# A bidirectional encoder layer on eight cores: two halves in residue order against one pass of three stages in token order

## The chip, the cores and the metric

The kernel runs on all 8 NeuronCores of one Trainium2 chip. Every core works on 4096 tokens of its own and recomputes what it needs of its neighbours' tokens: its window of x has 6144 rows, 1024 of them halo on each side. No data passes between cores. The metric is the device time in microseconds of the slowest core.

## The reference

```python
hn = rmsnorm(x, norm_g)
q, k, v, z_a, hc, gb, gc, z_b, g = split(hn @ w_in)      # widths 3 x 1536, then 5 x 512, then 2048
for gi, dil in enumerate((1, 4, 16)):                    # 8 heads of 64 per group
    # each query sees the keys at distances dil * j, |j| <= 64, with an ALiBi bias
    out[gi], lse[gi] = banded_attention(q, k, v, dil)
attn = sum(softmax(lse)[gi] * out[gi])
a = (silu(z_a) * attn) @ w_attn_out                      # 512 -> 1024
conv = centred depthwise convolution of width 3 of gc * hc
c = (silu(z_b) * gb * conv) @ w_conv_out                 # 512 -> 1024
merged = sigmoid(g_a + b) * a + sigmoid(g_c + b) * c
y = rmsnorm(x + merged @ w_o, final_g)
```

The model width is 1024. The tokens are one sequence of 16384 and two of 8192.

## The kernel before

The kernel is written on the five instruction queues directly. A helper records every instruction with the resources it reads and writes, and puts in the semaphore waits; each engine runs its own list in order. So the order in which the Python code emits instructions is the order on each engine. Most operations of VectorE (DVE), ScalarE (ACT) and GpSimd (POOL) have a line of their own; projections share `proj_fm` (matmul at L373), ACT copies out of PSUM share L366, and all DMAs L176. x tiles and outputs go on SP's queue, the weights, which are cast from f32 to bf16 on the way, on POOL's.

A core handles its 4096 tokens in two halves of 2048. The normalised, transposed window of one half, `hnT` (8 x 4096 columns of bf16), holds the tokens in residue order: tokens with the same remainder modulo 16 stand together, 256 per remainder. Loads of x with a row step of 16 put them there. The stages, once per half, are:

- **Norm** (`p1_stages`): per tile of 128 tokens a load, a square with sum on ACT (`rms_stat`, L385), two small POOL operations, the scaling on DVE (L432), eight transposes on TensorE (L438) and a copy into `hnT`. Half 0 does this for 32 tiles ahead of everything else.
- **Attention** (`phase2`): 12 units, one for each of 4 head pairs and 3 groups. `att_stages` gives each unit eight items: scores (L750), exponential (L758), multiplication with a table of bias and mask (L762), product with values and ones (L780) and accumulation. Between the items the pieces of `proj_pieces` project queries, keys and values for the next unit. Group 2 projects values tile by tile with `hnT` as the stationary operand (L672); groups 0 and 1 project them like keys and transpose them (L618, L692). Group 0 comes first and writes the accumulator, groups 1 and 2 add on DVE. After group 2 `finalize_parts` divides by the denominators and applies the SiLU gate.
- **Convolution** (`phase3a`) and **gates** (`phase3b`): wide projections of 512 columns; results stay in SBUF (`gattn`, `gconv`, `mergedV`).
- **Output** (`p3_stages`): 16 tiles; in half 0 mixed with the norm of the 16 tiles that half 1 still lacks, the other half of `hnT` being moved along by four DVE copies (L1120). Barriers stand before the attention and before the output.

The order of the mixed pipelines comes from times that are written into the code:

```python
return [(0, L), (1, S), (3, N), (6, E)] if h == 0 else [(0, L), (1, S), (3, N), (4.5, E)]
```

Load, square, scaling with transposes, and copy of tile i are issued at i plus these numbers, sorted.

Of the kernel before, what the change touches and what calls it, by code (L numbers as in the profile page):

```python
# [17 lines left out]
WIN = 4096  # L18
LW = 256
XROWS = 6144  # L20
EPS = 1e-6
# [4 lines left out]
X_BYTES = 84224  # L26
NWS = 8
# [8 lines left out]
def _tile_off(g):  # L36
    idx = np.arange(128)
    if g == 0:
        return 16 * (idx % 8) + idx // 8
    if g == 1:  # L40
        return 4 * (idx % 32) + idx // 32
    return idx

def _etab():
    sl = _slopes()
    out = np.zeros((24, 128, 256), np.float32)
    for g in range(3):
# [146 lines left out]

def build_program():
# [12 lines left out]
    cbf_d = nc.dram_tensor("cbf", [128, 512], BF16, kind="ExternalInput")  # L208
    et_d = nc.dram_tensor("etab", [24 * 128, 256], BF16, kind="ExternalInput")
    y_d = nc.dram_tensor("y", [TOK_CORE, D], F32, kind="ExternalOutput")  # L210

    import contextlib
    es = contextlib.ExitStack()
    with es:
# [888 lines left out]
        for f_ in first_loads:  # L1103
            f_()
# [130 lines left out]
```

How the kernel before makes its waits and increments, by code:

```python
                def body(e):  # L1153
                    for (wl, fn, tok, inc) in E.prog:
                        wl2 = [(sem[sname], rank[sname][v] if sname in rank else v) for (sname, v) in wl]
                        emb = None
                        if EMBED_WAIT and wl2 and kind in EMBED_WAIT and inc != 16:
                            emb = wl2.pop()
                        for (sh, v) in wl2:
                            e.wait_ge(sh, v)
                        ins = fn(e)
                        if emb is not None:
                            ins._wait_ge(emb[0], emb[1])
                        if tok is not None:
                            if tok[0] in rank:
                                if tok[1] in rank[tok[0]]:
                                    ins.then_inc(sem[tok[0]], 1)
                            else:
                                ins.then_inc(sem[tok[0]], inc)
                    if kind == "sp":
                        for sname, v in final_waits.items():
                            e.wait_ge(sem[sname], v)
                        for k2 in ("pe", "act", "dve", "pool"):
                            E2 = B.engs[k2]
                            if E2.count:
                                e.wait_ge(sem[E2.semname], rank[E2.semname][E2.count])
```

The softmax here doesn't subtract the row's maximum and nothing guards it: scores larger than these inputs give would overflow.

## Time and profile before

| | |
|---|---|
| time, median of 3 runs | 1803.38 us (1803.29 to 1804.26) |
| span of the profiled execution, slowest core | 1800.1 us |
| spans of the eight cores | 1783.9 to 1800.1 us |
| TensorE busy | 1632.2 us (91%) |
| VectorE busy | 954.4 us (53%) |
| ScalarE busy | 737.0 us (41%) |
| DMA, mean over the span | 62 GB/s |

The span goes from the first to the last instruction on the slowest core; the time of a run also holds what lies around it, 3.3 us between this span and the median. PE is TensorE's matmul side, PEld its weight loads, which overlap the matmuls. The end of a matmul is modelled in the profile, so starts are the safer thing to read in it.

### The profile page before, as it was taken

The page shows a single profiled execution, that of the slowest core. Times are in us where ns is not written, and L with a number is a line of the kernel's source. Part 1 is how long each engine was busy: PE and PEld are TensorE (multiplying, and loading weights), DVE is VectorE, ACT ScalarE, POOL GpSimd, SP SyncE. Part 2 cuts the span into 40 slices and gives each one's busy share as a digit, 9 for nine tenths or more (in the row PEclk, how much of TensorE's full clock was granted, in tenths as well). Part 3 has the DMA queues.
Part 4 walks back from the last instruction along what each step waited for, and adds up shares of the span by engine and source line. Part 5 has one row for each costly group of instructions (what it writes and reads, how often), then busy time and mean ns, then how long its engine had stood idle before and what let it go on. Part 6 is the DMA issues. An engine that isn't in the chain of part 4 may idle for free.

```text
span 1800.1 us, 30600 instructions; the slowest of 8 cores (1783.9 to 1800.1 us)
## 1 busy us (share of the span) xinstructions
PE 1632.2 (91%) x12270; PEld 894.3 (50%) x12328; DVE 954.4 (53%) x1490; ACT 737.0 (41%) x1385; POOL 246.7 (14%) x328
## 2 busy tenths in 40 slices
PE   2699999999897999999777998998999899999997
PEld 2356556556564444444333564565655644444443
DVE  4724654835748564433662347366474675633446
ACT  5654563564544112222353635546356421122222
POOL 5700010000100111000343000001000010100011
PEclk9999999999998999999998999999999999999999
DMA  9731041321311453221999313204204143522248
GB/s 257 180 46 19 10 48 19 36 21 13 36 19 30 53 47 36 24 24 30 253 284 127 34 13 39 25 7 50 20 3 46 13 65 36 48 24 27 34 123 275
DMA packets 177838, 112.23 MB, mean 62 GB/s; under 512 B 152480, under 2 KB 158752, under 8 KB 177696
## 3 DMA queue, kind: packets, MB, share of 16 engines
q0 software_dynamic: 154176, 46.15, 25.8%
q1 hardware_dynamic: 23520, 64.12, 11.6%
q8 instruction: 97, 1.59, 0.4%
q14 instruction: 45, 0.37, 0.1%
HBM read 139.61 MB, written 16.78 MB: 87 GB/s over the span
## 4 chain that ended last, share of the span: by engine, by line
PE 70%; DVE 10%; DMA 8%; ACT 5%; issue 4%; POOL 2%; SPq 0%; POOLq 0%; ACTq 0%; DVEq 0%
PE ps L373 52%; PE ps L672 6%; PE ps L1050 6%; DMA X<-xw 5%; PE ps L780 4%; DMA y<-X 3%; PE ps L750 2%; DVE X L839 2%; ACT X L758 2%; POOL stat L390 1%; DVE X L762 1%; ACT X L366 1%; DVE X L795 1%; DVE X L844 1%; DVE X L841 1%
## 5 line engine op out<-in xcount | busy, mean ns | idle before, releaser
L373 PE MATMUL ps<-hnT,wbf 128*128 128x512 bf16 (+4 forms) x5488 | 1096.3, 354 | 9.3 <-DVE X L834 3.9
L373 PEld LDWEIGHTS ps<-hnT,wbf 128*128 128x128 bf16 x5504 | 499.8, 99 | 528.2 <-issue 28.1
L762 DVE TENSOR_TENSOR X<-X,et 128x512 bf16<-128x512 bf16 x384 | 159.1, 424 | 317.5 <-ACT X L758 300.5
L366 ACT ACTIVATE X<-ps 128x512 bf16<-128x512 f32 (+3 forms) x384 | 194.7, 512 | 296.0 <-PE ps L373 281.4
L176 POOL DMA_DIRECT2D wbf<-w_in x144 | 132.0, 925 | 1156.0 <-PE ps L373 916.2
L758 ACT ACTIVATE X<-ps 128x512 bf16<-128x512 f32 x384 | 207.5, 598 | 118.3 <-PE ps L750 116.4
L780 PE MATMUL ps<-X 128*128 128x128 bf16 x1536 | 119.6, 222 | 45.7 <-DVE X L762 32.7
L385 ACT ACTIVATE X<-X 128x1024 bf16<-128x1024 f32 x80 | 84.3, 1053 | 117.4 <-DMA X<-xw 66.9
L487 PE MATMUL ps<-wbf,X 128*128 128x512 bf16 x500 | 116.4, 389 | 13.3 <-DVE X L1076 7.2
L780 PEld LDWEIGHTS ps<-X 128*128 128x128 bf16 x1536 | 89.7, 99 | 71.4 <-DVE X L762 41.5
L1064 ACT ACTIVATE X<-ps,cf 128x512 f32<-128x512 f32 x64 | 44.1, 690 | 181.8 <-DVE X L1073 108.9
L672 PE MATMUL ps<-wbf,hnT 128*128 128x128 bf16 x2048 | 118.3, 219 | 0.0
L672 PEld LDWEIGHTS ps<-wbf,hnT 128*128 128x128 bf16 x2048 | 115.7, 98 | 1.9
L1073 DVE SCALAR_TENSOR_TENSOR X<-X,ps 128x512 f32<-128x512 f32 x64 | 43.7, 683 | 136.3 <-PE ps L1050 136.3
L438 PE MATMUL ps<-cbfs,X 128*128 128x128 bf16 x384 | 43.7, 284 | 70.3 <-DVE X L432 66.2
L487 PEld LDWEIGHTS ps<-wbf,X 128*128 128x128 bf16 x512 | 50.4, 100 | 74.2 <-issue 14.0
L750 PE MATMUL ps<-X 64*128 64x128 bf16 x1536 | 76.8, 220 | 10.0 <-ACT X L758 9.2
L390 POOL TENSOR_TENSOR stat<-stat,cf 128x1 f32<-128x1 f32 x80 | 75.2, 940 | 18.3 <-DVE cf L306 11.7
L438 PEld LDWEIGHTS ps<-cbfs,X 128*128 128x128 bf16 x384 | 33.2, 128 | 84.1 <-ACT X L385 25.8
L1070 DVE SCALAR_TENSOR_TENSOR X<-X,ps 128x512 f32<-128x512 f32 x64 | 43.8, 684 | 56.7 <-PE ps L1050 56.7
L676 DVE CAST X<-ps 128x512 bf16<-128x512 f32 x64 | 44.3, 692 | 55.6 <-PE ps L672 55.6
L987 ACT ACTIVATE X<-ps 128x512 f32<-128x512 f32 x32 | 19.1, 597 | 132.2 <-PE ps L373 81.6
(60 smaller groups left out, 1234.3 us busy)
## 6 DMA issues: line engine op xcount, KB each, us to landing
X<-xw SPq DMA_DIRECT2D x80, 512.0 KB, 7.9
wbf<-w_in POOLq DMA_DIRECT2D x144, 256.0 KB, 6.2
y<-X SPq DMA_DIRECT2D x32, 512.0 KB, 6.6
wbf<-w_o POOLq DMA_DIRECT2D x16, 256.0 KB, 4.2
et<-etab SPq DMA_DIRECT2D x24, 128.0 KB, 2.2
X<-w_ao POOLq DMA_DIRECT2D x2, 1024.0 KB, 9.9
X<-w_co POOLq DMA_DIRECT2D x2, 1024.0 KB, 9.6
X<-gvec SPq DMA_DIRECT2D x2, 512.0 KB, 9.5
```

Of the source, the lines that this page charges most:

```text
L176: E.prog.append((wl, lambda e: e.dma_start(out=out, in_=in_), tok, 16))
L366: return op("act", lambda e: e.activation(out=out, in_=in_, func=AF.Copy), reads=reads, writes=writes)
L373: fns.append(lambda e, kt=kt: e.matmul(bv.cols(0, n), lhsT=w_lhsT(s, kt), rhs=hnT.ap(kt * WIN + rhs_start, rhs_dims), start=(kt == 0), sto ...
L385: op("act", lambda e: e.activation(out=junk_ap, in_=src_ap, func=AF.Square, accum_out=stat.cols(c0, 1)), reads=[src_res], writes=[junk_res ...
L390: op("pool", lambda e: e.tensor_tensor(out=stat.cols(c0 + 2, 1), in0=stat.cols(c0 + 1, 1), in1=cf.cols(CF_MH, 1), op=ALU.pow), reads=[r, R ...
L487: fns.append(lambda e, dt_=dt_, nh=nh, bv=bv: e.matmul(bv.cols(0, 512), lhsT=mergedV.cols(dt_ * NOWN + r16 * 128, 128), rhs=wbf.cols(dt_ * ...
L672: fns.append(lambda e, tt=tt, kt=kt, p0=p0: e.matmul(bv.cols(tt * 128, 128), lhsT=hnT.cols(kt * WIN + p0, 128), rhs=w_lhsT(sv, kt), start= ...
L750: fns.append(lambda e, b2=b2, t=t, kt_=kt_, bi=bi, bv=bv, hh=hh: e.matmul(bv.cols(b2 * 256 + t * 128, 128), lhsT=ktV[par].cols(kt_ * 128, ...
L758: op("act", lambda e, bv=bv, hh=hh: e.activation(out=prv.cols(hh * 512, 512), in_=bv.cols(0, 512), func=AF.Exp, scale=0.125), reads=[R_ban ...
L762: op("dve", lambda e, hh=hh, eoff=eoff: e.tensor_tensor(out=prv.ap(hh * 512, [[256, 2], [1, 256]]), in0=prv.ap(hh * 512, [[256, 2], [1, 25 ...
L780: fns.append(lambda e, b2=b2, t=t, kt_=kt_, hh=hh: e.matmul(bv.cols(hh * 256 + b2 * 128, 128), lhsT=vbV[par].cols(kt_ * VB_T + 64 * hh, 12 ...
L1050: fns.append(lambda e, ct=ct: e.matmul(bv.cols(0, 512), lhsT=wv.cols(ct * D + dt_ * 128, 128), rhs=gv_.cols(ct * NOWN + cc * 512, 512), st ...
```

## The change

`hnT` grows to the core's whole window, 8 x 6144 columns in natural token order, and every stage runs once over all of it.

1. **Norm with convolution.** 48 norm tiles in the order 7 to 40, 0 to 6, 41 to 47. The convolution is cut into 32 steps (`conv_step`, 4 channel tiles by 8 chunks of 512 tokens), and after each step `p1_until` issues a stretch of the norm's instructions, 1.36 tiles' worth. Each step projects HC, GC, ZB and GB; SiLU is now one ACT function. The result goes to DRAM (`gc_s`).
2. **Attention by head pair.** 24 units: head pair, then half, then group 2, 1, 0. `hnT` being in token order, the permutation by residue now happens where ACT copies queries and keys out of PSUM (strided reads or writes), and values of all groups are projected tile by tile with a strided `hnT` operand as stationary weights: step 1, 4 or 16 elements. Keys and values that both halves of a head pair need are computed in half 0, saved to DRAM (`k_s`, `v_s`) and loaded in half 1. Group 2 comes first and its accumulator write is an ACT copy with a step of 16; groups 1 and 0 add on DVE. The gated result goes to DRAM (`ga_s`). The pieces of the next unit are spread evenly over the eight items.
3. **Gates and output.** 8 chunks of 512 tokens: per chunk the gated arrays are loaded from DRAM and eight `merge_step`s run, each two gate projections (2 x 8 matmuls) and two branch projections (2 x 4), over a ring of six banks. Between them, one chunk behind, one output tile after every second step (`out_mm`: 16 matmuls into banks 6 and 7, then the DVE sum and the norm). The last four output tiles stand alone at the end. All 16 gate weight blocks stay in SBUF, and `w_o` is loaded once.

The barriers, the value transposes, the moving copies and the second half's reload of convolution, gate and output weights are gone. The stages of the old form are all removed; here are the core lines of the new one, moved left:

```diff
+    ga_d = nc.dram_tensor("ga_s", [4 * 128, TOK_CORE], BF16)
+    gc_d = nc.dram_tensor("gc_s", [4 * 128, TOK_CORE], BF16)
+    KOV = (1, 4, 16)
+    k_d = [nc.dram_tensor("k_s%d" % g, [128, KOV[g] * 128], BF16) for g in range(3)]
+    v_d = [nc.dram_tensor("v_s%d" % g, [128, KOV[g] * VB_T], BF16) for g in range(3)]
...
+order = list(range(7, 41)) + list(range(0, 7)) + list(range(41, 48))
...
+    return [(0, 0, L), (1, 1, S), (2.2, 2, N), (3, 3, E)]
...
+def p1_until(t):
+    while p1pos["i"] < len(p1ev) and p1ev[p1pos["i"]][0] <= t:
+        p1ev[p1pos["i"]][3]()
+        p1pos["i"] += 1
...
+    b_hc, b_gc, b_zb, b_gb = abank(), abank(), abank(), abank()
+    proj_fm(b_hc, w_hc, s, 512)
+    act_copy(hcs.v.base, bank(b_hc).cols(0, 512), [R_bank[b_hc]], hcs.r)
+    proj_fm(b_gc, w_gc, s, 512)
+    op("dve", lambda e: e.tensor_tensor(out=U.v.cols(2, 512), in0=bank(b_gc).cols(0, 512), in1=hcs.v.base,
+                                        op=ALU.mult), reads=[R_bank[b_gc]] + hcs.r, writes=U.r)
+    proj_fm(b_zb, w_zb, s, 512)
+    op("act", lambda e: e.activation(out=sz.v.base, in_=bank(b_zb).cols(0, 512), func=AF.Silu),
+       reads=[R_bank[b_zb]], writes=sz.r)
+    proj_fm(b_gb, w_gb, s, 512)
+    op("dve", lambda e: e.tensor_tensor(out=GZ.v.cols(1, 512), in0=bank(b_gb).cols(0, 512), in1=sz.v.base,
+                                        op=ALU.mult), reads=[R_bank[b_gb]] + sz.r, writes=GZ.r)
+    a0 = 1 if c == 0 else 0
+    n = 513 - a0 if c == 7 else 512 - a0
+    cw0, cw1, cw2 = (cf.cols(CF_CW + ct * 3 + k_, 1) for k_ in range(3))
+    cav = ca.v.cols(0, n)
+    op("dve", lambda e: e.tensor_scalar(out=cav, in0=U.v.cols(a0 + 1, n), scalar1=cw1, scalar2=None, op0=ALU.mult),
+       reads=U.r + [R_const], writes=ca.r)
+    op("dve", lambda e: e.scalar_tensor_tensor(out=cav, in0=U.v.cols(a0, n), scalar=cw0, in1=cav,
+                                               op0=ALU.mult, op1=ALU.add), reads=U.r + ca.r, writes=ca.r)
+    op("dve", lambda e: e.scalar_tensor_tensor(out=cav, in0=U.v.cols(a0 + 2, n), scalar=cw2, in1=cav,
+                                               op0=ALU.mult, op1=ALU.add), reads=U.r + ca.r, writes=ca.r)
+    op("dve", lambda e: e.tensor_tensor(out=gcs.v.cols(0, n), in0=cav, in1=GZ.v.cols(a0, n), op=ALU.mult),
+       reads=ca.r + GZ.r, writes=gcs.r)
+    if c < 7:
+        dve_copy(U.v.cols(0, 2), U.v.cols(512, 2), U.r, U.r)
+        dve_copy(GZ.v.cols(0, 1), GZ.v.cols(512, 1), GZ.r, GZ.r)
+    o0 = 512 * c - 1 + a0
+    dma("sp", "d_gc%d" % k, bass.AP(gc_d, ct * 128 * TOK_CORE + o0, [[TOK_CORE, 128], [1, n]]),
+        gcs.v.cols(0, n), reads=gcs.r, writes=R_gcd[max(c - 1, 0):c + 1])
...
+p1_until(0)
+conv_wload(0)
+load_consts()
+dma("sp", "d_gb", gb_.v.base, bass.AP(gvec, 0, [[0, 128], [1, D]]), writes=R_gb)
+p1_until(4)
+conv_wload(1)
+p1_until(6)
+conv_wload(2)
+conv_wload(3)
+p1_until(7)
+stepi = 0
+for sc in range(4):
+    for ct in range(4):
+        for c in (2 * sc, 2 * sc + 1):
+            conv_step(ct, c)
+            stepi += 1
+            if stepi == 1:
+                p1_until(11.5)
+            else:
+                p1_until(11.5 + (stepi - 1) * 1.36)
+        if sc == 3 and ct == 0:
+            wahead(3)
+        if sc == 3 and ct == 1:
+            wahead(4)
+p1_until(1e9)
...
+units = [(hp, h, g) for hp in range(4) for h in range(NHALF) for g in (2, 1, 0)]
...
+        if nload:
+            dma("sp", "d_kl%d" % par, kt.v.cols(0, nload * 128), k_d[g].ap(), reads=[R_kd[g]], writes=ksub(0, nload))
+            dma("sp", "d_vl%d" % par, vb.v.cols(0, nload * VB_T), v_d[g].ap(), reads=[R_vd[g]], writes=vsub(0, nload))
...
+    def vpiece(t0, n):
+        def run():
+            bk = next_pbank()
+            bv = bank(bk)
+            fns = []
+            lo, hi = 10 ** 9, 0
+            wf, wr = w_slot(sv)
+            for tt in range(n):
+                t = t0 + tt
+                if g == 0:
+                    p0 = ks + 128 * t
+                elif g == 1:
+                    p0 = ks + 512 * (t // 4) + t % 4
+                else:
+                    p0 = ks + 2048 * (t // 16) + t % 16
+                lo, hi = min(lo, p0), max(hi, p0 + 127 * d + 1)
+                for kk in range(8):
+                    fns.append(lambda e, tt=tt, kk=kk, p0=p0: e.matmul(
+                        bv.cols(tt * 128, 128), lhsT=hnT.ap(kk * WT + p0, [[d, 128]]),
+                        rhs=wf(kk), start=(kk == 0), stop=(kk == 7)))
+            pe_group(fns, reads=wr + hres(lo, hi), writes=[R_bank[bk]])
+            dve_copy(vb.v.ap(t0 * VB_T, [[VB_T, n], [128, 2], [1, 64]]),
+                     bv.ap(0, [[128, n], [64, 2], [1, 64]]), [R_bank[bk]], vsub(t0, n))
+        return run
+    if g == 0:
+        if h:
+            kl = [kpiece(128 + 512 * c) for c in range(4)]
...
+            kl = [kpiece(512 * c) for c in range(4)] + [kpiece(2048, 128)]
+    else:
+        kl = [kpiece(c) for c in range(nload // 4, nt // 4)]
+    vl = [vpiece(t0, min(4, nt - t0)) for t0 in range(nload, nt, 4)]
+    pieces += kl + vl
...
+    def save_piece():
+        t0 = nt - nov
+        dma("sp", "d_ks%d" % g, k_d[g].ap(), kt.v.cols(t0 * 128, nov * 128), reads=ksub(t0, nov), writes=[R_kd[g]])
+        dma("sp", "d_vs%d" % g, v_d[g].ap(), vb.v.cols(t0 * VB_T, nov * VB_T), reads=vsub(t0, nov), writes=[R_vd[g]])
+    if h == 0:
+        pieces.append(save_piece)
...
+    if g == 2:
...
+        act_copy(av_.ap(4 * quad + 2 * j, [[NOWN, 2], [1, 2], [16, 128]]),
+                 bv.ap(0, [[256, 2], [128, 2], [1, 128]]), [R_bank[ob]], acc_.r)
...
+    if g == 1:
+        av, ares = av_.ap(quad + 1024 * j, [[NOWN, 2], [4, 256]]), acc_.r
+    else:
+        av, ares = av_.ap(512 * quad + 256 * j, [[NOWN, 2], [1, 256]]), acc_res(quad)
...
+def out_tick(last=False):
+    i = done["mm"]
+    out_mm(i)
+    done["mm"] += 1
+    if done["fin"] < i:
+        out_fin(done["fin"])
+        done["fin"] += 1
+    if i + 2 < 32:
+        x3_load(i + 2)
...
+for c in range(8):
...
     for dt_ in range(8):
+        merge_step(c, dt_)
+        if c > 0 and dt_ % 2 == 1:
+            out_tick()
+    if c + 2 < 8:
+        load_chunk(c + 2)
+for _ in range(4):
+    out_tick()
+out_fin(done["fin"])
```

## Rows read from the trace of the kernel before

**Rows 1.** The page: engines' busy time, and TensorE's granted clock in 40 slices.
```profile
PE 1632.2 (91%) x12270; PEld 894.3 (50%) x12328; DVE 954.4 (53%) x1490; ACT 737.0 (41%) x1385; POOL 246.7 (14%) x328
...
PEclk9999999999998999999998999999999999999999
```

**Rows 2.** Windows by stage: length, busy per engine, clock, DMA share, GB/s.
```profile
0.00:82.00 82.00, 32.78 (x257) 24.73 (x258) 50.74 (x50) 52.50 (x81) 58.01 (x76) 1.00 0.83 227
82.00:569.40 487.40, 456.16 (x4357) 277.87 (x4366) 257.01 (x493) 242.37 (x493) 34.53 (x40) 0.98 0.26 28
569.40:859.00 289.60, 283.45 (x1339) 128.60 (x1352) 144.00 (x186) 65.64 (x104) 30.43 (x35) 0.99 0.34 38
859.00:958.80 99.80, 68.65 (x377) 33.18 (x384) 62.90 (x52) 50.11 (x80) 45.41 (x71) 0.90 0.92 264
958.80:1444.90 486.10, 453.83 (x4357) 276.67 (x4366) 256.83 (x492) 241.96 (x492) 35.17 (x41) 0.98 0.29 30
1444.90:1732.40 287.50, 280.95 (x1341) 127.99 (x1354) 144.22 (x186) 66.00 (x105) 30.42 (x35) 0.99 0.35 38
1732.40:1800.10 67.70, 56.43 (x251) 25.24 (x256) 38.68 (x32) 18.40 (x32) 12.72 (x32) 0.93 0.78 256
```

**Rows 3.** TensorE's timeline in attention: start, length, instructions, idle before.
```profile
150.84 0.40 PE L750 MATMUL ps<-X 64*128 64x128 bf16 x8
151.17 0.62 PE L780 MATMUL ps<-X 128*128 128x128 bf16 x8
151.62 5.34 PE L373 MATMUL ps<-hnT,wbf 128*128 128x512 bf16 x24
156.90 0.40 PE L750 MATMUL ps<-X 64*128 64x128 bf16 x8
```

**Rows 4.** Windows of two head pairs (half 0), and of one unit.
```profile
109.43:230.47 121.04, 116.53 (x1112) 70.50 (x1113) 61.52 (x121) 61.56 (x126) 5.28 (x7) 0.99 0.20 22
230.47:350.52 120.05, 113.67 (x1093) 69.18 (x1094) 67.27 (x127) 61.09 (x125) 8.75 (x11) 0.99 0.24 26
186.56:230.47 43.91, 41.06 (x324) 22.30 (x322) 31.27 (x51) 23.50 (x46) 0.03 (x1) 0.96 0.03 10
```

**Rows 5.** TensorE's timeline at the end of half 0's attention.
```profile
541.98 0.62 PE L780 MATMUL ps<-X 128*128 128x128 bf16 x8
...
559.22 1.03 PE L780 MATMUL ps<-X 128*128 128x128 bf16 x8 [4.15 <-DVE X L762]
...
568.56 1.03 PE L780 MATMUL ps<-X 128*128 128x128 bf16 x8 [3.76 <-DVE X L762]
```

**Rows 6.** Groups by form: count, busy us, mean ns, idle before.
```profile
L672 PE MATMUL ps<-wbf,hnT 128*128 128x128 bf16 x2048 | 118.3, 219 | 0.0
...
L672 PEld LDWEIGHTS ps<-wbf,hnT 128*128 128x128 bf16 x2048 | 115.7, 98 | 1.9
...
L432 DVE SCALAR_TENSOR_TENSOR X<-X,stat 128x1024 bf16<-128x1024 f32 x48 | 61.4, 1281 | 12.2 <-POOL stat L390 10.9 <-DMA X<-gvec 1.2
...
L993 DVE TENSOR_TENSOR X<-ps,X 128x512 f32<-128x512 f32 x32 | 22.1, 691 | 1.1
...
L1011 DVE SCALAR_TENSOR_TENSOR X<-X,cf 128x1920 f32<-128x1920 f32 x8 | 17.7, 2218 | 0.3
...
L1009 DVE TENSOR_SCALAR X<-X,cf 128x2048 f32<-128x2048 f32 x8 | 10.3, 1286 | 0.3
```

**Rows 7.** TensorE's timeline in the mixed stage.
```profile
859.41 7.07 PE L487 MATMUL ps<-wbf,X 128*128 128x512 bf16 x32 [3.58 <-DVE X L1076]
871.86 8.55 PE L487 MATMUL ps<-wbf,X 128*128 128x512 bf16 x31 [5.38 <-DVE X L494]
...
949.27 1.01 PE L438 MATMUL ps<-cbfs,X 128*128 128x128 bf16 x8 [4.41 <-DVE X L432]
...
958.85 9.41 PE L373 MATMUL ps<-hnT,wbf 128*128 128x512 bf16 x32 [2.36 <-DMA wbf<-w_in]
```

**Rows 8.** TensorE's timeline at the start.
```profile
20.64 2.14 PE L438 MATMUL ps<-cbfs,X 128*128 128x128 bf16 x16 [20.64 <-DVE X L432]
```

More of the change, by code:

```diff
@@ L193, in barrier, with __init__ @@
         self.epoch = ep
+class Buf:
+    def __init__(self, view, res):
+        self.v = view
+        self.r = res
 def build_program():
@@ L300, in build_program, with mrg @@
+        fgV = View(et_t[:, 0:2048].bitcast(F32))
+        R_mrg = [[Res() for _ in range(8)] for _ in range(2)]
+        def mrg(m, dt_):
+            return hnT.cols(dt_ * WT + m * 512, 512)
         CF_HB, CF_CW, CF_FL, CF_BG, CF_MH = 0, 16, 28, 32, 48
@@ new lines, in wload @@
+        def wload(sname, dst, col, res):
+            src = bass.AP(w_in, col, [[INW, 128], [128 * INW, 8], [1, 128]])
+            dma("pool", sname, dst, src, writes=res)
+        wblocks = []
+        for hp in range(4):
+            for h in range(NHALF):
+                for g in (2, 1, 0):
+                    for c in (C_Q, C_K, C_V):
+                        wblocks.append(c + g * 512 + hp * 128)
+                wblocks.append(C_ZA + hp * 128)
+        for dt_ in range(4):
+            wblocks.append(C_G + dt_ * 128)
+            wblocks.append(C_G + 1024 + dt_ * 128)
@@ L810, in att_stages @@
+                        ov = bv.ap(0, [[256, 2], [1, 256]])
+                        op("dve", lambda e: e.tensor_tensor(out=av, in0=ov, in1=av, op=ALU.add),
+                           reads=[R_bank[ob]] + ares, writes=ares)
                     items.append((stage_a, stage_b))
@@ new lines, in x3_load, with out_mm @@
+        def x3_load(i):
+            s = i % 4
+            dma("sp", "d_x3%d" % s, x3_[s].v.base, bass.AP(xw, (OWN0 + 128 * i) * D, [[D, 128], [1, D]]), writes=x3_[s].r)
+        out_st = {}
+        def out_mm(i):
+            c, r = divmod(i, 4)
+            m = c % 2
+            s = i % 4
+            x3 = x3_[s]
+            for nh in range(2):
+                bv = bank(6 + nh)
+                fns = []
+                for dt_ in range(8):
+                    fns.append(lambda e, dt_=dt_, nh=nh, bv=bv: e.matmul(
+                        bv.cols(0, 512), lhsT=hnT.cols(dt_ * WT + m * 512 + r * 128, 128),
+                        rhs=wo_[dt_].v.cols(nh * 512, 512), start=(dt_ == 0), stop=(dt_ == 7)))
+                pe_group(fns, reads=R_mrg[m] + [x for w_ in wo_ for x in w_.r], writes=[R_bank[6 + nh]])
+            op("dve", lambda e: e.scalar_tensor_tensor(out=x3.v.base, in0=bank(6, 2).base, scalar=0.5,
+                                                       in1=x3.v.base, op0=ALU.mult, op1=ALU.add),
+               reads=[R_bank[6], R_bank[7]] + x3.r, writes=x3.r)
+            out_st[i] = rms_stat(x3.v.base, x3.r)
```

1124 lines of the change are left out of this document (407 added, 717 removed).

## The prediction

> **What bounds the kernel now.** I first read the page. TensorE is busy 91% of the span, at a granted clock of 0.9 or more in all slices but one [rows 1], so the question is how many matmul columns the change removes and how often TensorE is kept waiting. The windows cut the span into seven stages [rows 2]: norm and transpose 82.0 us, attention 487.4, convolution and gates 289.6, a mixed stage of output and norm 99.8, attention 486.1, convolution and gates 287.5, output 67.7. In the attention and gate stages TensorE's busy time is 93 to 98% of the window. In the first stage it is 32.8 of 82, in the mixed one 68.7 of 99.8 with the DMA engines at 0.92: those two are where an overlap could pay.
>
> The timeline of TensorE inside attention gives its prices, start to start [rows 3]. Twenty-four matmuls of 512 columns take 151.62 to 156.90, so a group of eight takes 1.76. An item of attention (eight score and eight value matmuls) takes 150.84 to 151.62, 0.78 us. The 2048 value projections of 128 columns take 118.3 us [rows 6], 0.462 for the eight of one tile. From one memset of group 1's value buffer (L567) to the next, a head pair in one half takes 121.0 us, the next one 120.1: 241.1 us for two [rows 4].
>
> **Attention, by its parts.** Before, a head pair and half projects 6144 query, 8832 key, 2048 gate (ZA) columns and 4736 value columns (groups 0 and 1) through eight matmuls each: 21760/512 x 1.76 = 74.8 us. The 32 value tiles of group 2 add 14.8, the 37 transposes of values 37 x 0.058 = 2.1, the 24 items 18.7: 110.4 us, 220.8 for both halves. Against 241.1 that leaves 20.3 us of stalls.
>
> After, key and value tiles that the second half shares with the first come from DRAM: keys fall from 17664 to 14976 columns per head pair (17+20+32 tiles, then 16+16+16), and all values go tile by tile, 117 tiles, with no transposes. That is (12288+14976+4096)/512 x 1.76 = 107.8, plus 117 x 0.462 = 54.1, plus 48 x 0.78 = 37.4: 199.3 us. The saving is 21.5 per head pair, 86 us in all. The last unit of a half has nothing to project; from 541.98 to 569.4 it spends 27.4 us on 7 items (5.5) and four gate groups (7.0), so 15 us are lost, with waits such as the 4.15 us [rows 2, 5]. This now happens once, not twice. Attention becomes 487.4 + 486.1 - 86 - 15 = 872 us, if the other stalls stay; they could vary by 20.
>
> The halo stores and loads go on SP's queue, which in this stage carries only the mask tables and 0.1 MB stores; the DMA engines are busy 26 to 29% there [rows 2]. A load is needed two units after its store, so I price it at nothing; were that cover gone, it would cost one landing per unit of the second half.
>
> The values of groups 1 and 2 are now loaded as weights with a stride of 4 and 16 elements, in 36 and 48 of the 117 tiles. No row has a strided weight load. The nearest is the contiguous one of the same shape [rows 6]: 2048 matmuls in 118.3 us, the load (98 ns) wholly hidden. That is one bound, 0. The other is a load that nothing hides: 98 ns x 2688 loads = 263 us. I take 0, by the nearest row, and keep the rest as a rival. The Trainium skill, "SBUF — State Buffer", section "SBUF: two separate sides" and what follows it, says that SBUF has 16-byte lines and needs at least two hits on each for full speed. By it stride 4 is free and stride 16 is not; no run of before shows either.
>
> **Norm with convolution.** The columns are unchanged, 1024 matmuls of 512 and 48 x 8 transposes, and the stage aims to hide the norm behind them. The order of issue decides. Each `conv_step` emits its 32 matmuls and all its DVE work; only then does `p1_until` emit the norms (1.36 tiles a step, so at least one each time). On DVE the norm therefore queues behind the whole step, and on TensorE, in order, its transposes stand ahead of the next step's matmuls. The tail, from rows of like shape [rows 6]: after the last matmul (0.2 to its end) the product with the SiLU (0.6: the row's 0.69 less the overlap with its successor), the scaled copy (0.49, scaled from the 2048-column row), two multiply-adds of 512 at 0.75 (the rows of 1024 and 1920 columns, 1281 and 2218 ns, give 1.046 ns a column), a product 0.69, two copies of one and two columns, which no row shows (0.3, an estimate; 0 to 0.7 by the 512-column product), and the norm 1.28. So 5.1 us pass between the step's last matmul and its transposes. A warm step is 32 x 0.2175 = 7.0, plus 5.1, plus 0.45 for the transposes: 12.5. Ten of the 28 steps hold a second norm (+1.35), on average 0.5: 13.05 us.
>
> TensorE idles about 5 us each time. After idle 5.38 the next 31 matmuls took 8.55 us, against 6.8 at full clock; after 4.41 eight transposes took 1.01, where eight matmuls of 128 columns at full clock take 0.62 [rows 3]; at 958.85, after a stretch of short work, 32 matmuls took 9.41; only after 3.58 idle did 32 take the warm 7.07 [rows 7]. So I add 1.6 for the matmuls (1.7 and 2.3 in those rows) and 0.35 for the transposes: 15.0 us a step. The Trainium skill, "TensorE: Matmul & The Clock Gate", Part 1, says that idle stretches let the clock fall to its lower level and work brings it back; the trace agrees (4.15 and 4.41 us idle, then 1.03 and 1.01 us for eight matmuls).
>
> Sum: the first transposes start at 20.6 us today, behind the constants [rows 8], then five tiles at some 2.2 us and their copies: 35 before the first step; the step 7; a burst of five norms behind its tail 15; 28 x 15.0 = 420; three last steps without norm 21. Together 498 us. ScalarE has about 4.3 us of work a step. Should SiLU need another table than Square, its load falls between the HC copy and the ZB matmuls, where ScalarE waits anyway. The 16 weight blocks share the DMA engines with x tiles; later steps need only 1.36 tiles in 15 us.
>
> **Gates and output.** Before, 1288 wide matmuls took 289.6 us [rows 2], 0.225 each; the output's 256 were busy for 56.4 of 67.7, 0.220 each. Now 1536 x 0.225 = 345, and 512 x 0.220 = 113. The output uses only banks 6 and 7; between gate steps that is covered, but for the last four tiles three DVE reads of 1.2 us are exposed: 4. The tail behind the last matmuls is what it is today, 67.7 - 56.4 = 11. Together 473 us. The second half's reload of gate and output weights is gone (144 blocks of w_in become 112); POOL and DMA have room, so it gives nothing on the path. The re-read of the gated arrays, with x and y, is some 5 MB in 58 us, 90 GB/s, against the 264 of the mixed stage [rows 2].
>
> Total: 498 + 872 + 473 = 1843 us of span, where before has 1800.1. The median of before lies 3.3 us above its span; I forecast 1846 us.
>
> **The rivals.** *The clock holds.* If TensorE stays at its upper level, a step is 13.05 us, stage one 35 + 7 + 15 + 365 + 21 = 443, the time 1791 us: faster. For it: idle 3.58 left the clock up. Against it: all four idle stretches of 3.76 us and more in these rows, two in each group, were followed by slow matmuls [rows 5, 7]. It decides from 13.5 us a step ((455 - 78)/28), where the total meets 1803.
>
> *Strided weight loads are slow.* If each load at stride 16 takes the array's lower rate, about 107 ns where the pair now takes 57, it is 1536 x 50 ns = 77 us, and the time 1923. For it: the skill's rule on 16-byte lines, by which the same loads would slow. Against it: no row. With both strides unhidden it would be 2109.
>
> *DVE bounds the unit that finishes a head pair.* The unit that finishes a head pair now takes 43.9 us, 31.3 of them DVE's [rows 4], where TensorE's prices give 8 items (6.2), eight groups for queries and gates (14.1), 4352 columns of keys and values (15.0) and 17 transposes (1.0), 36.3: 7.6 us of stall. After, the one that runs ahead of the second half has the same DVE work and only 34.7 for TensorE. If both such units, and the shorter ones of the second half, lose another 7 us a head pair, the time is 1874. Against it: the pieces to project are now spread evenly over the items.
>
> **How the numbers follow.** Likeliest case, 0.43: 1846, with its own range 1815 to 1880. Clock holds, 0.22: 1791. Strided loads, 0.27: 1923. DVE, 0.08: 1874. The range 1785 to 1945 takes in all four and leaves out the far bound of the loads. A difference of 0.2%, 3.6 us, is about what can be told from none. Faster takes most of the clock's case and a little of the likeliest, 0.23; same 0.05; slower 0.72.
>
> **What would show it.** In the trace after: TensorE idle about 5 us before transposes, waiting for the DVE norm, 28 times, steps of 15 us and stage one ending near 498; a granted clock below 0.95 there; value matmuls of 128 columns at 57 ns in every unit (107 in group 2 for the second rival); head pairs near 219 us; the gate stage near 473. It is wrong if DVE reaches the norm sooner than the code's order says, if the clock stays up, or if strides cost.

## The result, and the profile after

The changed kernel takes 1901.16 us (median of 4 runs) against 1803.61 for the kernel before on the same chip (4 runs): 1.0543 times as long, 95% interval 1.0526 to 1.0559, or 97.6 us more. The forecast was 1846, 42.6 more. The direction and the range held; the change was more than twice the one forecast. In some executions here, of the kernel before and of the changed one too, part of the cores shows a lower granted clock and ends some per cent later; the ratios and intervals leave those executions out.

The page of the changed kernel, beside [rows 1]: TensorE's busy time fell by 30 us and its share from 91 to 84%. The columns saved in attention were priced at 86 us; matmuls and transposes at the low clock, priced at 28 x 1.95 us in stage one, take 55 of them back. The clock's row shows where it is not at its upper level of 2.4 GHz.

```profile
PE 1601.7 (84%) x12384; PEld 893.4 (47%) x12384; DVE 948.8 (50%) x1438; ACT 699.8 (37%) x1168; POOL 177.1 (9%) x286
...
PEclk9778888887899999998999989999888999999999
```

The windows of its three stages, which take the place of the seven of [rows 2]: length, busy time of each engine, granted clock, DMA share, GB/s.

```profile
0.00:514.70 514.70, 318.63 (x1537) 151.77 (x1538) 190.80 (x305) 135.08 (x215) 70.76 (x124) 0.83 0.38 71
514.70:1433.00 918.30, 836.45 (x8801) 540.78 (x8800) 538.17 (x867) 440.95 (x758) 70.60 (x81) 0.95 0.35 49
1433.00:1898.60 465.60, 446.58 (x2050) 200.82 (x2048) 219.79 (x267) 123.75 (x195) 35.77 (x81) 0.98 0.35 100
```

Against the sum: stage one 515 for 498 (+17), attention 918 for 872 (+46), gates and output 466 for 473 (-7). These make up the 56 us by which the span, 1898.6, misses the 1843 of the sum.

TensorE's timeline in stage one, and where the stage ends (start, length, instructions, idle before and its releaser):

```profile
234.03 1.01 PE L428 MATMUL ps<-cbfs,X 128*128 128x128 bf16 x8 [5.11 <-DVE X L422]
235.23 1.01 PE L428 MATMUL ps<-cbfs,X 128*128 128x128 bf16 x8 [0.19 <-DVE X L422]
236.03 8.98 PE L386 MATMUL ps<-hnT,X 128*128 128x512 bf16 x32
250.19 1.01 PE L428 MATMUL ps<-cbfs,X 128*128 128x128 bf16 x8 [5.18 <-DVE X L422]
...
490.81 24.02 PE L386 MATMUL ps<-hnT,X 128*128 128x1 bf16 x128
514.67 20.88 PE L386 MATMUL ps<-hnT,wbf 128*128 128x512 bf16 x96
```

DVE's timeline behind the last matmul of the step before those transposes (L501 to L513 are the step's tail, L422 is the norm that queues behind it):

```profile
229.10 0.69 DVE L501 TENSOR_TENSOR X<-ps,X 128x512 f32<-128x512 f32 x1 [2.73 <-PE ps L386]
229.71 0.48 DVE L507 TENSOR_SCALAR X<-X,cf 128x512 f32<-128x512 f32 x1
230.22 0.75 DVE L509 SCALAR_TENSOR_TENSOR X<-X,cf 128x512 f32<-128x512 f32 x1
...
232.41 0.27 DVE L379 COPY X<-X 128x2 f32<-128x2 f32 x2
232.60 2.48 DVE L422 SCALAR_TENSOR_TENSOR X<-X,stat 128x1024 bf16<-128x1024 f32 x2
```

The tail and the idle time are the forecast's, to a tenth: 5.11 and 5.18 us for 5.1. So are the steps. From 70.00, where the second step's matmuls start, to 490.81, where the last three follow one another, there are 28: 15.03 us each, for 15.0. The 17 us lie mostly at the ends: 13 before 70.00 (forecast 57) and 3 in the last three steps, which take 23.9 for 21 (the 128 matmuls of that row are their 96 and 32 of one column at the window's edges).

In attention one wait is new. The timelines of SP's queue, DVE and TensorE at the fourth unit of the first head pair:

```profile
655.24 0.70 SPq L163 DMA_DIRECT2D X<-v_s  x1
...
664.66 0.48 DVE L582 MEMSET X<- 128x512 f32 x1 [9.92 <-DMA X<-v_s]
...
655.06 0.62 PE L733 MATMUL ps<-X 128*128 128x128 bf16 x8
666.13 1.03 PE L733 MATMUL ps<-X 128*128 128x128 bf16 x8 [10.45 <-DVE X L713]
```

And the list of waits, who waited for whom: total us, times, longest:

```profile
PE ps L428 <- DVE X L422: 194.1, 46, 24.1
PE ps L733 <- DVE X L713: 56.2, 13, 12.4
DVE X L582 <- DMA X<-v_s: 43.8, 4, 11.7
```

The unit's first piece issues the loads of the halo keys and values and then clears the part of the value buffer that the unit will write. The load fills tiles 0 to 3 of group 1, 4 x 384 bytes; the kernel's bookkeeping counts in whole kilobytes, so the memset, which begins in the second kilobyte, is made to wait for the load to land. Behind that memset on DVE stand the products of the items (L713), and behind them, on TensorE, the value matmuls. It happens once a head pair, four times, always in group 1. The 16 tiles of group 2 fill whole kilobytes (16 x 384 bytes), so its memset shares none with the load; group 0's memset does share one, but VectorE reaches it at 696.82, 5.6 us after the load was issued (691.23), and these small loads take 2.1 us in the median; those of group 1 take 10.1.

The value matmuls that load their weights with a stride are the fourth thing to see. Groups by form, beside [rows 6], and then the windows of two units with those matmuls and loads (L636) alone:

```profile
L636 PE MATMUL ps<-wbf,hnT 128*128 128x128 bf16 x3744 | 228.3, 222 | 0.0
L636 PEld LDWEIGHTS ps<-wbf,hnT 128*128 128x128 bf16 x3744 | 222.3, 123 | 0.2
L749 DVE TENSOR_TENSOR X<-ps,X 128x512 f32<-128x512 f32 x128 | 112.6, 879 | 0.0
L376 ACT ACTIVATE X<-ps 128x512 f32<-128x512 f32 x96 | 87.5, 911 | 179.8 <-PE ps L386 107.6 <-DVE X L785 68.1 <-DVE X L484 3.9
```

```profile
696.82:726.97 30.15, 7.47 (x128) 7.23 (x128) 1.00 0.34 30
726.97:779.20 52.23, 16.44 (x256) 16.19 (x256) 1.00 0.12 35
```

A mean load takes 123 ns where the contiguous ones took 98, and 3744 matmuls are busy for 228.3 us, 61.0 ns each, for 57.8 in [rows 6]. In the second window, whose 256 are the next head pair's group 2 (stride 16), it is 64.2; in the first, whose 128 are group 0's and contiguous, 58.4. Nothing comes near 107. By source line, one load takes 98 ns in the median for group 0 (from 715.5 on), 113 for group 1 with its stride of 4 (from 686.5) and 148 for group 2 (from 753.0); group 1's matmuls are as short as group 0's (64 in 3.74 us).

### The profile page after: what moved, and what is told of

Read it like the earlier page. It is cut to its first block, busy times and chain, and to the rows that moved or that the text cites. A ratio compares the mean times of both kernels' runs of the same rounds, so it can differ in the third digit from the quotient of the medians.

```text
span 1898.6 us, 30275 instructions; the slowest of 8 cores (1880.8 to 1898.6 us)
## 1 busy us (share of the span) xinstructions
PE 1601.7 (84%) x12384; PEld 893.4 (47%) x12384; DVE 948.8 (50%) x1438; ACT 699.8 (37%) x1168; POOL 177.1 (9%) x286
## 4 chain that ended last, share of the span: by engine, by line
PE 74%; DVE 16%; DMA 4%; issue 3%; ACT 2%; SPq 0%; DVEq 0%; POOL 0%; POOLq 0%; ACTq 0%
PE ps L386 44%; PE ps L636 10%; PE ps L934 6%; PE ps L960 6%; PE ps L733 4%; PE ps L700 2%; DVE X L422 2%; DMA X<-v_s 2%; DVE X L780 2%; PE ps L428 2%; DMA X<-xw 1%; DVE X L713 1%; DVE X L511 1%; DVE X L509 1%; DVE X L773 1%
## 5 line engine op out<-in xcount | busy, mean ns | idle before, releaser
L386 PE MATMUL ps<-hnT,wbf 128*128 128x512 bf16 (+2 forms) x3072 | 721.6, 390 | 4.4 <-DVE X L775 3.7
L386 PEld LDWEIGHTS ps<-hnT,wbf 128*128 128x128 bf16 x3072 | 299.3, 102 | 355.3 <-issue 60.3
L376 ACT ACTIVATE X<-ps 128x512 bf16<-128x512 f32 (+2 forms) x320 | 214.2, 678 | 383.6 <-PE ps L386 309.9
L713 DVE TENSOR_TENSOR X<-X,et 128x512 bf16<-128x512 bf16 x384 | 157.6, 423 | 235.6 <-ACT X L709 228.9
L386 PE MATMUL ps<-hnT,X 128*128 128x512 bf16 (+1 forms) x1088 | 252.8, 391 | 0.0
L636 PE MATMUL ps<-wbf,hnT 128*128 128x128 bf16 x3744 | 228.3, 222 | 0.0
L636 PEld LDWEIGHTS ps<-wbf,hnT 128*128 128x128 bf16 x3744 | 222.3, 123 | 0.2
L733 PE MATMUL ps<-X 128*128 128x128 bf16 x1536 | 121.8, 224 | 72.5 <-DVE X L713 56.2
L386 PEld LDWEIGHTS ps<-hnT,X 128*128 128x128 bf16 x1088 | 107.8, 104 | 134.3 <-issue 29.6
L934 PE MATMUL ps<-X 128*128 128x512 bf16 x512 | 121.9, 381 | 0.0
L960 PE MATMUL ps<-X,hnT 128*128 128x512 bf16 x512 | 115.8, 379 | 5.8 <-DVE X L964 5.8
L749 DVE TENSOR_TENSOR X<-ps,X 128x512 f32<-128x512 f32 x128 | 112.6, 879 | 0.0
L495 DVE TENSOR_TENSOR X<-ps,X 128x512 f32<-128x512 f32 x32 | 22.2, 692 | 174.3 <-PE ps L386 137.4
```

The source lines that it names most:

```text
L376: return op("act", lambda e: e.activation(out=out, in_=in_, func=AF.Copy), reads=reads, writes=writes)
L386: fns.append(lambda e, kt=kt: e.matmul(bv.cols(c0, n), lhsT=wf(kt), rhs=hnT.cols(kt * WT + t0, n), start=(kt == 0), stop=(kt == 7)))
L636: fns.append(lambda e, tt=tt, kk=kk, p0=p0: e.matmul(bv.cols(tt * 128, 128), lhsT=hnT.ap(kk * WT + p0, [[d, 128]]), rhs=wf(kk), start=(kk ...
L713: op("dve", lambda e, hh=hh, eoff=eoff: e.tensor_tensor(out=prv.ap(hh * 512, [[256, 2], [1, 256]]), in0=prv.ap(hh * 512, [[256, 2], [1, 25 ...
L733: fns.append(lambda e, b2=b2, t=t, tk=tk, hh=hh: e.matmul(bv.cols(hh * 256 + b2 * 128, 128), lhsT=vb.v.cols(tk * VB_T + 64 * hh, 128), rhs ...
L749: op("dve", lambda e: e.tensor_tensor(out=av, in0=ov, in1=av, op=ALU.add), reads=[R_bank[ob]] + ares, writes=ares)
```

## The experiments

All are edits of the changed kernel; ratios are to the kernel before on the same chip.

**The memset ahead of the loads.** In the first piece of a unit:

```
-  if nload: dma(... kt ... k_d[g] ...); dma(... vb ... v_d[g] ...)
   memset / pattern copy of tiles nload..nt
+  if nload: dma(... kt ... k_d[g] ...); dma(... vb ... v_d[g] ...)
```

> The ones memset and the mask copy of a unit's value buffer are issued before the two halo loads instead of behind them; nothing else changes. Theory A (the halo load sits under the memset: they share a 1 KB granule of the bookkeeping, the memset of group 1 in half 1 waits 10 to 12 us for the load, four times, and DVE's queue and then TensorE wait with it): the four waits of the memset on v_s disappear, the unit of 48.9 us falls to about 38, the time falls by 40 to 50 us to about 1855. Rival B (that unit is bound by DVE's own finishing work, the load only fills a gap): under 10 us, about 1895.

Measured: 1859.78 us, 1.032 (1.0301 to 1.0338): 41 us less than the changed kernel, as the waits on the list say. The memset's wait for `v_s` is gone from the list, and the row of the value matmuls' wait is now

```profile
PE ps L733 <- DVE X L713: 12.1, 15, 3.7
```

12.1 us instead of 56.2. The unit of 48.9 us (from the memset at 615.73 to the one at 664.66) takes 39.05 (618.89 to 657.94), where 38 was expected. The order of two statements costs 41 us.

**The transposes after the step's matmuls.** The norm is split: DVE's part stays where it was, the transposes and their copy come 1.4 tiles later in the written order, behind the next step's matmuls.

```
-  return [(0, 0, L), (1, 1, S), (2.2, 2, N), (3, 3, E)]
+  return [(0, 0, L), (1, 1, S), (2.2, 2, N), (3.6, 2.5, T), (4.4, 3, E)]
-  p1_until(7) ... p1_until(11.5) ... p1_until(11.5 + (stepi - 1) * 1.36)
+  p1_until(8.5) ... p1_until(12.9) ... p1_until(12.9 + (stepi - 1) * 1.36)
```

> Norm with convolution: the eight transposes of a norm tile are taken out of the norm's slot and issued 1.4 tiles later, so that the next convolution step's 32 matmuls stand ahead of them on TensorE. Theory A (the order of issue costs about 5 us of idle per step, 28 times, and the clock falls in them): steps shrink from 15.4 to about 7.7 us, stage one from 515 to 300, the time to about 1685. Rival B (the stage is bound by the work of DVE, ScalarE or the DMA engines, whatever the order): stage one stays above 450 us, the time above 1835. Rival C (order decides, but DVE's 5.7 us a step and its waits on PSUM let steps fall only to about 10): 1750.

Measured: 1732.33 us, 0.9623 (0.9593 to 0.9654), 169 us less, where 1685 was expected. TensorE's timeline:

```profile
209.64 0.61 PE L430 MATMUL ps<-cbfs,X 128*128 128x128 bf16 x8
210.09 7.07 PE L386 MATMUL ps<-hnT,wbf 128*128 128x512 bf16 x32
217.00 0.61 PE L430 MATMUL ps<-cbfs,X 128*128 128x128 bf16 x8
221.51 1.04 PE L430 MATMUL ps<-cbfs,X 128*128 128x128 bf16 x8 [3.90 <-ACT hnT L376]
222.34 8.12 PE L386 MATMUL ps<-hnT,wbf 128*128 128x512 bf16 x32
```

A step is 7.35 us where nothing is late: there both the idle time and the low clock are gone, which shows that the order of issue made them. Stage one ends at 357.51 for 514.67 (the first projection of attention), 157 of the 169 us; most of the others lie in the memset's wait of the edit before, 33.1 us here for 43.8. The gain fell short of the expectation because the next thing is late in its place: x tiles. ScalarE's square waits 148.5 us in all for its x tile (29 times, in the list of waits), ScalarE is in order, and the copies out of the transposes, for which TensorE then waits (33.6 us), stand behind it.

**TensorE kept busy.** Behind each of the first 29 steps, 20 matmuls of 512 columns whose result nothing reads: work is added. (The counter is raised before it is compared, and the trace has 12964 matmuls for 12384.) An earlier run of the same kernel (six executions, 1839.73 to 2093.03 us, median 1892.10) gave no comparison; its lowest time agrees.

```
+  if cstep["i"] <= 29:
+      b_x = abank()
+      pe_group([20 matmuls of w_gb x hnT into b_x], ...)
```

> The same kernel as the one with 20 extra matmuls a step, for a time that undisturbed runs give. Theory A: about 1840. Rival B: 1901.

Measured: 1839.41 us, 1.0201 (1.0183 to 1.0218), granted clock 0.973 to 0.977 for 0.929 to 0.937: 62 us less, with 580 more matmuls.

```profile
204.08 0.61 PE L428 MATMUL ps<-cbfs,X 128*128 128x128 bf16 x8 [0.86 <-DVE X L422]
204.53 7.07 PE L386 MATMUL ps<-hnT,wbf 128*128 128x512 bf16 x32
211.43 4.48 PE L505 MATMUL ps<-hnT,wbf 128*128 128x512 bf16 x20
216.70 0.61 PE L428 MATMUL ps<-cbfs,X 128*128 128x128 bf16 x8 [0.79 <-DVE X L422]
...
464.24 20.88 PE L386 MATMUL ps<-hnT,wbf 128*128 128x512 bf16 x96
```

The step is 12.6 us with one norm and 13.9 with two; the norm is no sooner, so the difference is the price of the clock. Over the same 28 steps (70.83 to 442.72) the mean is 13.28 us for 15.03: 1.75 us a step. Stage one ends at 464.24 for 514.67, 50 of the 62 us. The other 12 lie behind it; the memset's wait, 37.2 us for 43.8, has part of them, and the rest is not resolved. Had the clock held by itself in stage one, as the first rival said, the changed kernel would have gained about these 50 us and still been slower than the kernel before.

**Both edits.** The memset first, and the late transposes.

> Memset ahead of the halo loads and late transposes together. If the two effects are independent, the gains add: 215 + 45 us, about 1640, below the kernel before. If one covers the other, less.

Measured: 1702.79 us, 0.9459 (0.9442 to 0.9475). Of the two gains of 41 and 169, 198 are there together; the missing 12 are about what late transposes alone had already taken from the memset's wait. The expectation missed by 63 for the same reason as that of late transposes; the square's wait for x tiles is 157.6 us.

**Norms after every second step.** Same norms, in half as many batches.

```
-  else:            p1_until(11.5 + (stepi - 1) * 1.36)
+  elif stepi % 2:  p1_until(11.5 + (stepi - 1) * 1.36)
```

> Norm with convolution: the norm's instructions are issued after every second step instead of every step, twice as many at a time; the transposes stay behind their norm, as in the changed kernel. Theory A (each batch costs the convolution's DVE tail, the first norm and a clock drop, some 7.5 us, and each further norm only 1.4): 14 batches in place of 28, so stage one loses 14 x 7.5 = 105 us less 14 x 1.4 = 20 for the longer batches, the time about 1815. Rival B (the cost goes with the number of norm tiles, not of batches): no change, 1901.

Measured: 1868.75 us, 1.0372 (1.0346 to 1.0398), 32 us less and not 86: a miss.

```profile
223.18 1.03 PE L428 MATMUL ps<-cbfs,X 128*128 128x128 bf16 x8 [5.09 <-DVE X L422]
224.37 1.03 PE L428 MATMUL ps<-cbfs,X 128*128 128x128 bf16 x8 [0.16 <-DVE X L422]
228.89 1.01 PE L428 MATMUL ps<-cbfs,X 128*128 128x128 bf16 x8 [3.48 <-DVE X L422]
229.70 15.29 PE L386 MATMUL ps<-hnT,X 128*128 128x512 bf16 x64
```

The tail's 5.09 is paid half as often, but a batch often has a third norm, and this one's square stands on ScalarE behind the copies of the first two: 3.48 us more of idle time (7.35 where x is late too), at the low clock.

**Contiguous weight loads.** Groups 1 and 2 take 128 neighbouring tokens in place of every 4th or 16th; their values are those of other tokens.

```
-  lhsT=hnT.ap(kk * WT + p0, [[d, 128]])
+  lhsT=hnT.cols(kk * WT + p0, 128)
```

> Attention: the value projections load their stationary operand from 128 neighbouring tokens instead of tokens 4 or 16 apart, so the values of groups 1 and 2 are those of other tokens; all counts and shapes stay. Theory A (the strided load is nearly hidden; the changed kernel's 3744 matmuls are busy 228.3 us, 61.0 ns each against 57.8 before): 57.8 ns, a gain of at most 12 us, time about 1890. Rival B (stride 16 costs much more where loads pile up): over 30 us.

Measured: 1892.64 us, 1.0504 (1.0483 to 1.0524): 8.5 us less.

```profile
L636 PE MATMUL ps<-wbf,hnT 128*128 128x128 bf16 x3744 | 218.5, 219 | 0.0
L636 PEld LDWEIGHTS ps<-wbf,hnT 128*128 128x128 bf16 x3744 | 211.5, 98 | 0.2
```

The loads are back at 98 ns and the matmuls 9.8 us less busy. That is the whole of the second rival, for which 77 us was forecast. The Trainium skill, "SBUF — State Buffer", section "SBUF: two separate sides" and what follows it, wants at least two hits on each 16-byte line for full bandwidth. Stride 16 in bf16 gives one, and the trace agrees in direction: 148 ns a load for 98, and 64.2 ns a matmul for 58.4. Stride 4 gives two, and its loads still take 113 ns, which the rule does not give, but its matmuls are no slower. Most of the slower load stays behind the matmul before it.

**Contiguous accumulator.** Groups 1 and 2 write and add their outputs at neighbouring places in place of every 4th or 16th; the sums then mix tokens.

```
-  av_.ap(4 * quad + 2 * j, [[NOWN, 2], [1, 2], [16, 128]])      # group 2
+  av_.ap(512 * quad + 256 * j, [[NOWN, 2], [1, 256]])
-  av_.ap(quad + 1024 * j, [[NOWN, 2], [4, 256]])                # group 1
+  av_.ap(512 * quad + 256 * j, [[NOWN, 2], [1, 256]])
```

> Attention: group 2 writes and group 1 adds into the accumulator at neighbouring columns instead of columns 16 and 4 apart, so the sums mix tokens; counts and shapes stay. In the changed kernel group 1's DVE adds take 1.07 us instead of 0.68 and group 2's ScalarE copies 1.1 instead of 0.6. Theory A (both engines have room there): under 5 us. Rival B (these longer reads and writes delay exponentials and products and with them TensorE): 64 x 0.39 us on DVE and 64 x 0.5 on ScalarE come back, 20 us or more.

Measured: 1894.84 us, 1.0506 (1.0481 to 1.053), 6 us less, between the two theories. The interval overlaps the changed kernel's (1.0526 to 1.0559) at its edge, so the 6 is at the limit of what can be told.

```profile
L749 DVE TENSOR_TENSOR X<-ps,X 128x512 f32<-128x512 f32 x128 | 87.3, 682 | 0.0
L376 ACT ACTIVATE X<-ps 128x512 f32<-128x512 f32 x96 | 58.1, 605 | 183.5 <-PE ps L386 108.2 <-DVE X L785 71.2 <-DVE X L484 3.9
```

DVE's adds lose 25 us of busy time and ScalarE's copies 29, and at most some 6 of it is on the path.

**All three.** The memset first, the late transposes, and the x loads 2.5 tiles earlier in the written order.

```
-  return [(0, 0, L), ...
+  return [(-2.5, 0, L), ...
```

> Memset first, late transposes, and the loads of x issued 2.5 tiles earlier (the six x buffers allow it). With late transposes alone ScalarE waited 157.6 us for x in front of the squares, in 29 waits of up to 16.4. Theory A (the load, queued behind the convolution's store and used one tile later, is what still holds stage one, 317 us to the first attention item against some 250 of matmul work): 30 to 45 us less than memset first with late transposes, about 1665. Rival B (the waits lie beside TensorE's work): within 5 us of 1703.

Measured: 1648.59 us, 0.9147 (0.913 to 0.9163): 8.5% less than the kernel before, and the fastest of all. It is 54 us less than with two edits, where 30 to 45 was expected, and the square's wait for x tiles falls from 157.6 us (the wait of the run with two edits; late transposes alone had 148.5) to 20.6. Its windows by stage:

```profile
0.00:343.80 343.80, 295.17 (x1890) 154.32 (x1892) 198.65 (x319) 140.05 (x227) 73.18 (x126) 0.98 0.63 111
343.80:1196.00 852.20, 800.54 (x8486) 516.11 (x8486) 541.36 (x866) 437.46 (x752) 80.98 (x96) 0.98 0.36 52
1196.00:1645.90 449.90, 434.94 (x2012) 196.34 (x2010) 207.70 (x253) 119.67 (x189) 23.62 (x64) 0.99 0.33 100
```

The first boundary is the first item of attention here (L702), so the 344 stands against 551 in the changed kernel; the end of stage one as above, the first projection of attention, is at 307.04 for 514.67. DVE's busy time up to the boundary is 199 us, little more than the 191 of stage one before; it no longer stands in TensorE's way.

**Early loads alone.**

> The changed kernel with only the loads of x issued 2.5 tiles earlier. Theory A (there the step is set by the DVE tail, and ScalarE's waits for x lie beside it; only the burst after the first step gains): 5 to 15 us, about 1890. Rival B (late x tiles make up the part of stage one beyond my 498 us and more): over 25 us.

Measured: 1923.8 us (1916.3 to 1927.14), where 1890 was expected: 23 more than the changed kernel. For this run there is no interval; the median of the kernel before on its chip is 1800.66. Stage one in the changed kernel (core 3), then two stretches of it with the early loads on core 6, which has the longest span, and on core 2:

```profile
60.00:490.00 430.00, 276.92 (x1288) 129.95 (x1289) 165.30 (x265) 114.06 (x181) 49.33 (x88) 0.82 0.28 60
```

```profile
230.00:350.00 120.00, 83.42 (x324) 36.47 (x322) 40.68 (x66) 28.89 (x45) 8.26 (x20) 0.69 0.26 56
350.00:500.00 150.00, 99.52 (x445) 45.55 (x443) 57.41 (x92) 38.50 (x61) 19.56 (x34) 0.77 0.30 50
...
230.00:350.00 120.00, 78.01 (x337) 36.11 (x341) 45.88 (x75) 31.43 (x49) 11.62 (x22) 0.82 0.30 57
350.00:500.00 150.00, 101.48 (x443) 46.56 (x453) 53.52 (x85) 36.11 (x58) 16.95 (x32) 0.70 0.35 53
```

And TensorE's timeline on core 6:

```profile
231.64 10.06 PE L386 MATMUL ps<-hnT,X 128*128 128x512 bf16 x32
246.87 1.01 PE L428 MATMUL ps<-cbfs,X 128*128 128x128 bf16 x8 [5.18 <-DVE X L422]
247.68 10.45 PE L386 MATMUL ps<-hnT,X 128*128 128x512 bf16 x32
...
529.05 25.38 PE L386 MATMUL ps<-hnT,wbf 128*128 128x512 bf16 x96
```

The idle stretches are the same 5.11 to 5.18 us; the 32 matmuls behind them take 10.06 and 10.45 us on core 6 where they took 8.98 and 8.33. The added time is the clock's, but the rows speak against the idle stretches as its only cause. Until about 230 us core 6 runs at 0.82 like the changed kernel, and core 2 does so until 350. And the 96 matmuls after stage one, which follow one another without a gap, take 25.38 us on core 6 at a granted clock of 0.81 (532 to 556 us), as on five more cores, for 20.88 on cores 2 and 3 and on every core of the changed kernel. Something lowers the clock of this execution that begins at a different time on each core and goes on when TensorE is busy. Before it, the early loads are ahead: core 3, slow only from about 336 us on, starts the matmuls of the twelfth step at 216.64, for 220.91 on core 3 of the changed kernel. In all four executions some cores have a mean clock of 0.91 to 0.92; those at 0.935 or more end at 1874 to 1885, for 1881 to 1899 in the profiled execution of the changed kernel. So the 23 us are no price of the early loads that these rows show; if anything the loads gain, as theory A said.

**Norms after every second step, and early loads.**

> The norm after every second step, with the loads of x 2.5 tiles earlier. The run without early loads gave back only 32 us of the 85 that I expected; in it DVE waited 62.1 us for rstd, 13 times, up to 7.9, that is for squares of tiles loaded inside the same batch. Theory A (each batch costs the tail and a clock drop once, and the miss was the late load): 13 waits go, the time falls by another 45 to 55 us to about 1820. Rival B (a batch of three norms costs as much as three): within 10 us of 1869.

Measured: 1858.19 us, 1.0333 (1.029 to 1.0375), 10 less than without the early loads and 38 above theory A: a miss by the time. DVE's waits for rstd shrank (35.4 us in 14 waits up to 3.1, for 62.1 and 7.9) but did not go: the third norm still waits 3.4 us, behind ScalarE's copies and not behind a load. The cores differ: 0 to 3 end at 1822 to 1829, core 5 at 1855, and the same two steps' 64 matmuls take 15.09 us on core 3 and 18.42 on core 5, behind the same idle times. So the time is that of the cores whose clock fell as in the run before (0.78 from 60 to 490 us on cores 4 and 5, 0.84 on the others); on cores 0 to 3 theory A's 1820 is nearly met.

**Early loads with TensorE kept busy.** This asks whether the early loads cost anything beside the clock.

> The changed kernel with both edits at once: the x loads 2.5 tiles earlier, and the 20 matmuls of 512 columns that nothing reads behind each of the first 30 convolution steps (work added, results unused). Theory A, the early loads made the changed kernel slower only through the granted clock after each idle stretch: with TensorE kept busy they can't, and the time is at or a little below the 1839 of the kept-busy kernel, 1830 to 1840, with steps of 12.6 to 13.9 us. Theory B, the early loads cost something else, such as a transfer or a queue that they hold up: the time is about 23 us above the kept-busy kernel, near 1860, at the same clock of 0.97 to 0.98.

Measured: 1843.93 us, 1.0217 (1.0197 to 1.0237), clock 0.974 to 0.978. This is 4 us above theory A's range; beside the 1.0201 of the kept-busy kernel the intervals overlap, and 1860 is excluded. In the median of the cores stage one ends 4 us sooner (456.7 for 460.9). Kept busy, the early loads cost nothing that can be told, so theory B is out: no transfer or queue that they hold up takes 23 us. It does not show that the early loads lowered the clock in the run before. (The expectation says 30 steps; as above there are 29.)

## Why the prediction was right in direction and wrong in size

The prediction's parts, against what was measured:

- *Norm with convolution*: right in mechanism and in the price of a step. DVE's norm queues behind the step, TensorE idles 5.1 us and runs slowly after it; 28 steps of 15.03 us. Late transposes (-169 us) show the order as the cause, and the kept-busy matmuls price the clock at 1.75 us a step, for the 1.6 and 0.35 taken. The term that was too small is the start: the first step's matmuls began at 37.8 for 35 and took 9.8 for 7, the square of the burst's fourth norm waited 6.76 us for its x tile (on ScalarE, from 56.6 to 63.3), and the end of the burst moved from the 57 forecast to 70. With the last three steps, whose first 5 us have a granted clock of 0.51, +17 us. Two readings in the prediction are off and change nothing: the clock of the kernel before is below 0.9 in two of 40 slices, not one [rows 1], and the scaled copy's 0.49 us is not what its row gives in proportion (1.286 us by 512/2048, 0.32), though 0.48 was measured.
- *"A load is needed two units after its store, so I price it at nothing"*: this is the step that failed. The sentence asked whether the data would be late for its reader, and it is not. It did not ask what was written behind the load on the same buffer. The memset waits for its landing, 10 to 12 us, with DVE's whole queue behind it (43.8 us in four waits). The prediction had named the cost if the cover were gone, "one landing per unit of the second half", and it is one such landing per head pair, in group 1. Undone: -41 us; from the first projection of attention to the last group of eight ahead of the gate stage it is then 883 us (517.78 to 1400.79) for 925 (514.67 to 1439.58), so that the window of 918 becomes one of 876, for the 872 forecast.
- *The strides*: weight loads taken at 0 cost 8.5 us, the rival's 77 is refuted. The accumulator's strides were not in the sum at all, and cost some 6.
- *The first rival*, that the clock holds: refuted by the profile (0.83 in stage one). Its gain would have been about the 50 us of the kept-busy stage one, for the 55 forecast, and the time near 1850, not 1791, as the other terms were short too.
- *DVE bounds the unit that finishes a head pair*: that unit took 52.2 us (726.97 to 779.20), but with the memset first all of attention comes to 876 for the 872 forecast, which leaves no room for 7 us a head pair unless other stalls shrank; no run tests this rival by itself.
- *Gates and output*: 466 for 473. The wide matmuls ran somewhat better than 0.225 us each.

Of the 56 us by which the span missed, the memset accounts for 41, the strides for 14 or 15, the ends of stage one for 17 and the gates for -7; that is 10 more than 56. The other stalls of attention must then be smaller than the prediction kept them, within the 20 allowed; no run shows them apart. The runs remove one thing at a time, so the costs need not add exactly.

Open: what lowered the clock in the executions with the early loads. The rows show that it began at a different time on each core (0.75 to 0.78 from 60 to 490 us on cores 0 to 3, 6 and 7, 0.81 on cores 4 and 5) and went on in back-to-back matmuls, and not why, nor whether the edit has a part in it.

## What to carry to other kernels

When a load is priced at nothing because its reader comes late, look also for whoever writes to the same buffer next, with the grain in which the program tracks it: one memset behind a load cost more than all the strided accesses together. Where two chains share an in-order engine, what waits for the tail has to stand behind the next step's matmuls: the late transposes alone turned 5.4% slower into 3.8% faster, and with the memset first and the loads early the same arithmetic is 8.5% faster. (Issuing the norm on DVE ahead of the tail is the other way, and no run tried it.) A stall of TensorE of some 5 us cost its own length and 1.75 us more here, so remove the stall before anything else is tuned. And before a difference of 23 us is put down to an edit, look at each core's clock in a stretch that the edit does not touch.

## What the runs showed of the hardware that was not expected

- Weight loads with a stride, 128x128 bf16: 98 ns contiguous, 113 at stride 4, 148 at stride 16 (123 in the mean), but only 61.0 ns for a load and its matmul of 128 columns for 58.4 contiguous (218.5 us by 3744).
- float32 to strided places: a DVE add of 512 columns takes 879 ns in the mean of 128, half of them at stride 4 (1.08 us each), for 682 contiguous; a ScalarE copy 911 in the mean of 96, 64 of them at stride 16, for 605.
- Short stalls in every step keep the clock of a whole stage low: 0.82 with 5.1 us of idle time in every 15. 580 matmuls of which nothing is used made the kernel 62 us faster.
- TensorE can be slower at the same work in one execution than in another: 32 matmuls of 512 columns in 8.33 to 8.98 us, or in 10.06 to 10.45, behind 5.11 to 5.18 us of idle time, and 96 in a row in 20.88 or in 25.38 (granted clock 1.00 or 0.81), on cores of the same execution.
